# Three inner Strassen products per pair instead of two, in the four FFNs of a fused two-block kernel

## The chip, the cores and the metric

One core of one Trainium2 chip runs the whole kernel: an execution is one launch of one program. The metric is device time in microseconds. TensorE multiplies, VectorE, ScalarE and GpSimd work on tiles in SBUF (VectorE and ScalarE also in PSUM, where TensorE writes), and SyncE's and ScalarE's queues issue the transfers from HBM. All data are float32. The profile records each matmul as two instructions: four matmuls of 128x256, one product of the text, show as "x8".

## The reference, cut to what matters

Two blocks act on `x` of 512 tokens by 1024 features. The first is FFN, a mixer of attention and pooling, FFN; the second has two layers, each a mixer (attention with selected keys, then a state space model) and a convolved FFN. The change touches the four FFNs, here FFN0 to FFN3:

```
def swiglu(x, w1, w3, w2):
    return (jax.nn.silu(x @ w1) * (x @ w3)) @ w2
...
    h = h + 0.5 * swiglu(rms_norm(h, ffn1_norm[l]), ffn1_w1[l], ffn1_w3[l], ffn1_w2[l])
...
def conv_ffn(h, w_up, conv_w, conv_b, w_down):
    up = h @ w_up
    up = lax.conv_general_dilated(
        up, conv_w[:, None, :], window_strides=(1,), padding=[(CONV_W - 1, 0)],
        dimension_numbers=('NWC', 'WIO', 'NWC'), feature_group_count=2 * D_FF) + conv_b
    val, gate = jnp.split(up, 2, axis=-1)
    return (jax.nn.silu(gate) * val) @ w_down
```

FFN0 and FFN1 are `swiglu`, FFN2 and FFN3 `conv_ffn` with `CONV_W = 3`. The inner width `D_FF` is 2816. The second block also needs `silu(c) @ ada_w + ada_b` for its scales; that work lies in FFN0 and FFN1.

## The kernel before, in words

**The up projection by Strassen.** Everything is stored with features on the partitions. An FFN's 2816 columns (22 tiles of 128, `FC`) are taken in `NP = 11` pairs `p`. A pair has two weight slots `w`: `w = 0` and `w = 1` hold 256 columns of each of the two up matrices (or halves of `w_up`). Each slot's product with the tokens is a 2 by 2 block product in Strassen's form (Winograd's variant), so seven products `"P1"` to `"P7"` in place of eight; an outer product is `KC // 2 = 4` matmuls of a 128x128 weight block with 256 tokens. The sums of weight blocks that it needs (`combine`, four of 128x512 a slot, L624 to L629) are GpSimd's. The sums of token blocks (`h_mix_dve`) are made once for an FFN.

**The second level.** From the second pair on, two outer products of both slots share their tokens, so P6 (called `w = 2`) and P7 (`w = 3`), each for both slots at once, are again 2 by 2 products and again done by seven: an inner product is two matmuls with 128 tokens (`inner`, L746). Their weight sums are four of 128x256 each for GpSimd (`combine` with `inner_left`), their token sums `t1` to `t4` are VectorE's, once an FFN (`h_inner_mix`). P4 of both slots stays outer: two products of four matmuls.

**VectorE puts the results together.** In the first pair by `first_step` 1 to 5 for each slot, after that by `pair_step` 1 to 20, which read PSUM and add into the tiles `u` (P1 of both slots, copied by ScalarE as `first(p, w)`) and `act_t` (`quadrants`). Steps 1 to 8 need the first four inner products of each kind, and ScalarE's copies of the first inner products (`inner_copy_act`). TensorE's `(2, "P2")` waits for step 4, `(3, "P2")` for step 8. Each step adds one to the semaphore `quad`.

**Behind the steps** come, in FFN0 and FFN1, ScalarE's silu and two `product`s into `gT` (L1013, L1016) and four `ada_slab_dve` a pair, each a 128x1024 multiply and sum for the second block's scales (L1348). In FFN2 and FFN3 a pair has four tiles; each gets a `base` tap on ScalarE (L2599) and two more taps on VectorE (`earlier`, L2637 and L2640), then a silu and `product` (L2646). The taps of slot 0 are held in PSUM in pairs 1 to 9, those of slot 1 in SBUF (`rs`, `acc`).

**The down projection** (`strassen_down_pe`, L836) is Strassen's too in FFN0, FFN1 and FFN3. It needs four sums of the gated tiles of each pair `r` (`g_mix_dve`, L940 to L945): for pairs 0 to 7 they are made within the up projection, after the pair's last product; for pairs 8 to 10 behind it (`g_mix_last_dve`). FFN2 has a plain down projection (`down_pe`). The down weights of one quarter come in three slots (`GROUPS`: four, four and three pairs). For each slot TensorE does P1, P6, P7 and P5, then the next slot's.

**The weights** stream through a ring of four slots of 1 MB. A pair uses two; a slot is loaded anew when TensorE has passed the event in `FREES`, here `(w, "P3")` of its pair. Then GpSimd waits for the load and combines. The order of TensorE's products within a pair is written out by hand in `pair_steps`, that of the other engines in the functions named above; all meet through counting semaphores.

## Time and profile before

| what | value |
|---|---|
| median of 3 runs | 2671.56 us (2663.66 to 2671.83) |
| profiled execution, its own time | 2669.95 us |
| its span, first to last instruction | 2668.2 us |
| mean granted TensorE clock | 0.983 |
| busy TensorE | 2578.8 us, 97% |
| busy VectorE | 1681.1 us, 63% |
| busy GpSimd | 1232.2 us, 46% |
| busy ScalarE | 595.9 us, 22% |
| read from HBM | 255.14 MB |

The times are those of whole executions; the profile is of one of them, and the span leaves out what lies around the first and the last instruction. Busy shares are averages over stages, so a share says how full an engine is, not who waits for whom; the timeline and the waits say that.

### The profile page before, as it was taken

Reading aid. Unit: us, or ns where it says so; the run is one execution under the profiler, and the core shown is the slowest. Engines: PE = TensorE matmul, PEld = TensorE weight load, DVE = VectorE, ACT = ScalarE, POOL = GpSimd, SP = SyncE. Lnnn points to the kernel's source line nnn. Section 1 sums busy time; section 2 is a strip of 40 time slices with the busy share of each in tenths; the row PEclk is TensorE's granted clock in tenths of the full one; section 3 lists DMA queues with packets and bytes.
Section 4 is the critical chain, followed back from the end, with each engine's and each line's share of the span. In section 5 each row is a group of like instructions: output and inputs, shape, how many; then the busy total and the mean of one; then the engine's idle time right before and its main releaser. Section 6 shows DMA issues by size and latency. Waiting matters only on the chain.

```text
span 2668.2 us, 33470 instructions
## 1 busy us (share of the span) xinstructions
PE 2578.8 (97%) x12942; PEld 2056.1 (77%) x12942; DVE 1681.1 (63%) x2859; ACT 595.9 (22%) x1172; POOL 1232.2 (46%) x1128
## 2 busy tenths in 40 slices
PE   7999999999999999999999989999999699999999
PEld 6999889888467889886654567999644567899888
DVE  6776512588656887523498765677652875788721
ACT  2111001432201111002235642222202621222200
POOL 6666532440435677440000254677031884677642
PEclk9999999999999999999999999999999799999999
DMA  6555422221124555421122012223330422122222
GB/s 205 182 189 170 158 87 79 95 64 64 48 71 139 175 166 181 156 89 53 48 63 79 17 32 72 75 91 104 105 86 11 148 91 79 64 95 95 91 78 68
DMA packets 244062, 264.26 MB, mean 99 GB/s; under 512 B 31744, under 2 KB 226112, under 8 KB 243776
## 3 DMA queue, kind: packets, MB, share of 16 engines
q1 hardware_dynamic: 227968, 206.89, 24.5%
q10 hardware_dynamic: 15936, 55.22, 5.9%
q8 instruction: 104, 1.70, 0.3%
q14 instruction: 54, 0.44, 0.1%
HBM read 255.14 MB, written 6.29 MB: 98 GB/s over the span
## 4 chain that ended last, share of the span: by engine, by line
PE 88%; DVE 6%; POOL 2%; issue 2%; ACT 1%; DMA 0%; SPq 0%; DVEq 0%; ACTq 0%
PE ps L791 27%; PE ps L836 14%; PE ps L746 9%; PE ps L1615 6%; PE ps L589 6%; PE ps L2203 5%; PE ps L1434 3%; PE ps L3213 3%; PE ps L2238 2%; PE ps L1588 1%; PE ps L1744 1%; PE ps L1575 1%; POOL phase L3469 1%; PE ps L1158 1%; PE ps L2251 1%
## 5 line engine op out<-in xcount | busy, mean ns | idle before, releaser
L791 PE MATMUL ps<-hT,ring 128*128 128x256 f32 x2176 | 505.0, 381 | 7.9 <-DVE phase L1013 4.7
L791 PEld LDWEIGHTS ps<-hT,ring 128*128 128x128 f32 x2176 | 411.2, 191 | 67.5 <-issue 9.1
L624 POOL TENSOR_TENSOR ring<-ring 128x512 f32<-128x512 f32 (+1 forms) x124 | 168.7, 1360 | 552.5 <-DMA ring<-in_ffn_w 301.1
L836 PE MATMUL ps<-phase,ring 128*128 128x256 f32 x1848 | 400.1, 379 | 1.6 <-DVE phase L945 1.5
L836 PEld LDWEIGHTS ps<-phase,ring 128*128 128x128 f32 x1848 | 351.2, 190 | 50.0 <-DVE phase L945 2.3
L791 PE MATMUL ps<-phase,ring 128*128 128x256 f32 x1472 | 349.2, 381 | 6.2 <-DVE act_t L856 5.5
L791 PEld LDWEIGHTS ps<-phase,ring 128*128 128x128 f32 x1472 | 274.5, 191 | 41.6 <-DVE act_t L856 6.7
L627 POOL TENSOR_TENSOR ring<-ring 128x512 f32<-128x512 f32 (+2 forms) x204 | 237.6, 1165 | 0.0
L2561 POOL TENSOR_SCALAR phase<-phase 128x128 f32<-128x128 f32 (+3 forms) x64 | 33.4, 535 | 334.9 <-DVE phase L2530 334.9
L626 POOL TENSOR_TENSOR ring<-ring 128x512 f32<-128x512 f32 (+1 forms) x124 | 167.7, 1353 | 9.7
L629 POOL TENSOR_TENSOR ring<-ring 128x512 f32<-128x512 f32 (+1 forms) x124 | 171.1, 1380 | 0.0
L589 PE MATMUL ps<-phase,ring 128*128 128x512 f32 x352 | 152.3, 593 | 0.0
L882 DVE TENSOR_TENSOR act_t<-act_t,ps 128x128 f32<-128x128 f32 (+1 forms) x320 | 102.1, 349 | 69.1 <-PE ps L791 66.2
L2203 PE MATMUL ps<-hT,ring 128*128 128x512 f32 x320 | 140.1, 593 | 1.0 <-ACT hT L1310 0.5
L589 PEld LDWEIGHTS ps<-phase,ring 128*128 128x128 f32 x352 | 66.5, 190 | 81.5 <-issue 81.3
L2203 PEld LDWEIGHTS ps<-hT,ring 128*128 128x128 f32 x320 | 60.7, 190 | 78.0 <-issue 76.4
L1434 PE MATMUL ps<-phase,ring 128*128 128x256 f32 x448 | 99.4, 384 | 3.7 <-DVE phase L1404 3.6
L1348 DVE CUSTOM_DVE_ANT_0 phase<-phase,ps,vcol 128x1024 f32<-128x1024 f32 x80 | 101.9, 1273 | 0.0
L1615 PE MATMUL ps<-phase,ring 128*128 128x256 f32 x448 | 101.3, 379 | 0.0
L1434 PEld LDWEIGHTS ps<-phase,ring 128*128 128x128 f32 x448 | 86.0, 192 | 17.2 <-DVE phase L1404 4.5
L746 PE MATMUL ps<-phase,ring 128*128 128x128 f32 x640 | 96.1, 278 | 2.0 <-DVE u L882 2.0
L882 DVE TENSOR_TENSOR act_t<-u,ps 128x256 f32<-128x256 f32 (+1 forms) x120 | 44.9, 374 | 83.2 <-PE ps L791 52.2
(451 smaller groups left out, 4403.5 us busy)
## 6 DMA issues: line engine op xcount, KB each, us to landing
ring<-in_ffn_w SPq DMA_DIRECT2D x60, 1024.0 KB, 5.4
phase<-in_ada_w ACTq DMA_DIRECT2D x96, 512.0 KB, 3.5
ring<-in_ffn_w_up SPq DMA_DIRECT2D x44, 1024.0 KB, 5.0
ring<-in_w_in SPq DMA_DIRECT2D x19, 1024.0 KB, 5.2
ring<-in_attn_w_in SPq DMA_DIRECT2D x14, 1024.0 KB, 5.2
ring<-in_ffn_w_down SPq DMA_DIRECT2D x8, 1408.0 KB, 6.3
ring<-in_ssm_w_glu SPq DMA_DIRECT2D x8, 1024.0 KB, 5.7
ring<-in_ffn_w_down SPq DMA_DIRECT2D x8, 1024.0 KB, 5.1
```

The lines of the kernel that those rows point to most:

```text
L589: mm = pe.matmul(ps[:, (q % 2) * 2 + t, :], wtile(nd + 2 * q + s, c, FC // 2, t * P, (t + 1) * P), gT[:, f * T:(f + 1) * T], start=(f == 0 ...
L624: pool.tensor_tensor(s1, a21, a22, ALU.add).then_inc(combined, 1)
L626: pool.tensor_tensor(s2, s1, a11, ALU.subtract).then_inc(combined, 1)
L627: pool.tensor_tensor(a21, a11, a21, ALU.subtract).then_inc(combined, 1)
L629: pool.tensor_tensor(s4, a12, s2, ALU.subtract).then_inc(combined, 1)
L746: mm = pe.matmul(ps[:, inner_bank(w), at:at + P], left[:, c], tokens[:, c], start=(name == "P1" and c == 0), stop=(c == 1), skip_group_che ...
L791: mm = pe.matmul(ps[:, 4 * w + bank_of[name], 0:HALF], left[:, c], right[name](c), start=(opens and c == 0), stop=(c == KC // 2 - 1), skip ...
L836: mm = pe.matmul(ps[:, bank_of[name], 0:HALF], left[:, r - lo], right(name, r), start=(half == 0 and r == 0), stop=(r == NP - 1), skip_gro ...
L882: dve.tensor_tensor(dst, x, y, ALU.add).then_inc(quad, 1)
L1434: mm = pe.matmul(ps[:, out_bases(q) + banks[name], 0:HALF], left[:, c], right(name, c), start=(name in ("P1", "P6", "P7", "P5") and c == 0 ...
L1615: mm = pe.matmul(ps[:, bank, 0:HALF], left[:, c], right[name](c), start=(name in ("P1", "P6", "P7", "P5") and c == 0), stop=(c == KC // 2 ...
L2203: mm = pe.matmul(out, wtile(n, c, KC, t * P, (t + 1) * P), src(c), start=(c == 0), stop=(c == KC - 1))
```

## The change

The other products with shared tokens, P4 of both slots, become a third inner product (`w = 4`) from the second pair on. It takes PSUM bank 1, which the first inner product (`w = 2`) also uses, so each waits for VectorE's reads of the other. Its tokens are the outer token sum `t4` in `hx[:, 2]`; its own token sums are GpSimd's, once an FFN (`h_inner_last_pool`), its weight sums four more of 128x256 a pair. A pair has 25 steps: 17 to 21 and 24, 25 place the third product, two of the old steps go. Both slots of a pair are now freed by its very last product, `(4, "P3")`.

The other engines' orders change with it. In the first pair the token sums of the inner products are spread between the steps. The sums of gated tiles are made in pairs 3, 5, 7 and 9 for pairs 0 to 3, and for pairs 4 to 10 behind the up projection; TensorE waits for them at P6 instead of P1. Two of the four slabs of the first pair move to the down projection's second quarter. In FFN2 and FFN3 the taps are done tile by tile, that of `(w, i) = (0, 0)` before step 23 and the other three behind step 25. The rotation table's operations in FFN1 are spread one to a pair.

```diff
-INNER = (2, 3)
+INNER = (2, 3, 4)
...
-    order = [(0, "P1"), (1, "P1")] + [(w, name) for w in INNER for name in ("P1", "P6", "P7", "P5")]
-    order += [(0, "P5"), (0, "P2")] + [(2, name) for name in ("P2", "P4", "P3")] + [(1, "P5")]
-    order += [(3, name) for name in ("P2", "P4", "P3")]
-    return order + [(1, "P2"), (0, "P4"), (0, "P3"), (1, "P4"), (1, "P3")]
+    opening, closing = ("P1", "P6", "P7", "P5"), ("P2", "P4", "P3")
+    order = [(0, "P1"), (1, "P1")] + [(w, name) for w in (2, 3) for name in opening]
+    order += [(0, "P5"), (0, "P2")] + [(2, name) for name in closing] + [(1, "P5"), (1, "P2")]
+    order += [(3, name) for name in closing] + [(4, name) for name in opening]
+    return order + [(0, "P3"), (1, "P3")] + [(4, name) for name in closing]
...
-                put(n + 2 * b + w, e + EVENTS[k]["up", b, w, "P3"])
+                put(n + 2 * b + w, e + EVENTS[k]["up", b, 4 if b else w, "P3"])
...
+        def h_inner_last_pool(pool, k):
+
+            b11, b12, b21, b22 = inner_right(4)
+            t1, t2, t4 = inner_sums(k, 4)[0]
+            pool.wait_ge(h_mixed, 4 * k + 4)
+            pool.tensor_tensor(t1, b12, b11, ALU.subtract).then_inc(last_mixed, 1)
+            pool.wait_ge(last_mixed, 4 * k + 1)
+            pool.tensor_tensor(t2, b22, t1, ALU.subtract).then_inc(last_mixed, 1)
+            pool.wait_ge(last_mixed, 4 * k + 2)
+            pool.tensor_tensor(t4, b21, t2, ALU.subtract).then_inc(last_mixed, 1)
+            pool.wait_ge(tile_done, TILE0[f"ffn{k}"] + EVENTS[k]["up", 0, 1, "P4"])
+            pool.tensor_tensor(b12, b22, b12, ALU.subtract).then_inc(last_mixed, 1)
...
                             for r in range(lo, hi):
                                 if q == 0 and name == "P1":
+                                    pe.wait_ge(gated, FC * k + 2 * r + 2)
+                                if q == 0 and name == "P6":
                                     pe.wait_ge(g_mixed, G_MIXED0[k] + 4 * (r + 1))
...
-            if step in (17, 19):
-                w = (step - 17) // 2
-                done(w, "P4")
-                add(g[w], g[w], ps[:, 4 * w, 0:HALF])
-            if step in (18, 20):
-                w = (step - 18) // 2
+            if step == 17:
+                dve.wait_ge(in_copied, copies + 3)
+                add(v4, v4, inner(4, 3, 4))
+            if step == 18:
+                after(17)
+                add(g[0][:, P:], g[0][:, P:], v4)
+            if step == 19:
+                x = g[1].rearrange("p (s t) -> p s t", s=2)
+                add(x, x, v4.unsqueeze(1).to_broadcast([P, 2, P]))
+            if step in (20, 21):
+                after(step - 1)
+                add(g[1][:, P:], g[1][:, P:], inner(4, 2, 3) if step == 20 else inner(4, 1, 2))
+            if step in (22, 23):
+                w = step - 22
                 done(w, "P3")
                 add(quadrants[w][:, HALF:2 * HALF], halves[:, w, :], ps[:, 4 * w + 3, 0:HALF])
+            if step == 24:
+                done(4, "P3")
+                add(g[0], g[0], inner(4, 0, 2))
+            if step == 25:
+                add(g[1][:, 0:P], g[1][:, 0:P], inner(4, 2, 3))
...
+        G_MIX_AT = (3, 5, 7, 9)
+
         def g_mix_last_dve(dve, k):
 
-            dve.wait_ge(tile_done, TILE0[f"ffn{k}"] + EVENTS[k]["up", NP - 1, 1, "P4"])
-            for r in range(8, NP):
+            dve.wait_ge(tile_done, TILE0[f"ffn{k}"] + EVENTS[k]["up", NP - 1, 4, "P3"])
+            for r in range(len(G_MIX_AT), NP):
                 g_mix_dve(dve, k, r)
...
-        SLAB_BEHIND = (8, 9, 16)
+        SLAB_BEHIND = (8, 9, 21, 25)
...
-                for step in range(9, 19):
+                for step in range(12, 23):
                     pair_step(dve, k, p, step)
-                earlier(p, 0)
-                pair_step(dve, k, p, 19)
-                pair_step(dve, k, p, 20)
-            earlier(NP - 1, 1)
+                tile_taps(p, 0, 0)
+                for step in range(23, 26):
+                    pair_step(dve, k, p, step)
+                tile_taps(p, 1, 0)
+            for w in range(2):
+                tile_taps(NP - 1, w, 1)
+            product(NP - 1, 0)
             product(NP - 1, 1)
-            product(NP - 1, 0)
```

Three places show how the instructions now stand. The first is TensorE's queue at the end of a pair of FFN0, before: behind P2 of slot 1 come P4 and P3 of slot 0, P4 and P3 of slot 1, each four matmuls.

```order
L791 MATMUL ps<-hT,ring 128x256 [waits first_products_copied]
L791 MATMUL ps<-hT,ring 128x256 x3
L791 MATMUL ps<-phase,ring 128x256 [waits silu_done]
L791 MATMUL ps<-phase,ring 128x256 x3
L791 MATMUL ps<-hT,ring 128x256 [waits weights_combined,quadrant_steps]
L791 MATMUL ps<-hT,ring 128x256 x3
L791 MATMUL ps<-phase,ring 128x256 [waits gated]
L791 MATMUL ps<-phase,ring 128x256 x3
L791 MATMUL ps<-hT,ring 128x256 [waits weights_combined,quadrant_steps]
L791 MATMUL ps<-hT,ring 128x256 x3
```

And now: the end of the third inner product's opening (its P7 and P5), P3 of both slots, and its closing P2, P4 and P3 (two matmuls each).

```order
L774 MATMUL ps<-phase,ring 128x128 [waits weights_combined]
L774 MATMUL ps<-phase,ring 128x128
L774 MATMUL ps<-sq,acc 128x128 [waits weights_combined]
L774 MATMUL ps<-sq,acc 128x128
L814 MATMUL ps<-hT,ring 128x256 [waits weights_combined,quadrant_steps]
L814 MATMUL ps<-hT,ring 128x256 x3
L814 MATMUL ps<-hT,ring 128x256 [waits weights_combined,quadrant_steps]
L814 MATMUL ps<-hT,ring 128x256 x3
L774 MATMUL ps<-phase,ring 128x128 [waits quadrant_steps]
L774 MATMUL ps<-phase,ring 128x128
L774 MATMUL ps<-acc,ring 128x128 x2
```

What moved: both outer P4 left, and an inner P2 that waits for step 21 stands between the last outer product and the pair's end.

The second place is VectorE's queue at the end of a pair of FFN2, before: steps 17 and 18, the four taps of slot 0 (in PSUM), steps 19 and 20, the four taps of slot 1.

```order
L882 TENSOR_TENSOR act_t<-act_t,ps 128x256 [waits tile_done]
L882 TENSOR_TENSOR act_t<-u,ps 128x256 [waits tile_done]
L2637 SCALAR_TENSOR_TENSOR ps<-act_t,vcol,ps 128x511 [waits conv_base]
L2640 SCALAR_TENSOR_TENSOR ps<-act_t,vcol,ps 128x510 [waits conv_taps]
L2637 SCALAR_TENSOR_TENSOR ps<-act_t,vcol,ps 128x511 [waits conv_base]
L2640 SCALAR_TENSOR_TENSOR ps<-act_t,vcol,ps 128x510 [waits conv_taps]
L882 TENSOR_TENSOR act_t<-act_t,ps 128x256 [waits tile_done]
L882 TENSOR_TENSOR act_t<-u,ps 128x256 [waits tile_done]
L2637 SCALAR_TENSOR_TENSOR rs<-act_t,vcol,rs 128x511 [waits conv_base]
L2640 SCALAR_TENSOR_TENSOR rs<-act_t,vcol,rs 128x510 [waits conv_taps]
L2637 SCALAR_TENSOR_TENSOR acc<-act_t,vcol,acc 128x511 [waits conv_base]
L2640 SCALAR_TENSOR_TENSOR acc<-act_t,vcol,acc 128x510 [waits conv_taps]
```

And now: step 22, one tile's taps, steps 23 to 25, and then three tiles' taps; two rows of products follow in both orders.

```order
L914 TENSOR_TENSOR act_t<-u,ps 128x256 [waits tile_done]
L2703 SCALAR_TENSOR_TENSOR ps<-act_t,vcol,ps 128x511 [waits conv_base]
L2706 SCALAR_TENSOR_TENSOR ps<-act_t,vcol,ps 128x510 [waits conv_taps]
L914 TENSOR_TENSOR act_t<-u,ps 128x256 [waits tile_done]
L914 TENSOR_TENSOR act_t<-act_t,ps 128x256 [waits tile_done]
L914 TENSOR_TENSOR act_t<-act_t,ps 128x128
L2703 SCALAR_TENSOR_TENSOR acc<-act_t,vcol,acc 128x511 [waits conv_base]
L2706 SCALAR_TENSOR_TENSOR acc<-act_t,vcol,acc 128x510 [waits conv_taps]
L2703 SCALAR_TENSOR_TENSOR ps<-act_t,vcol,ps 128x511 [waits conv_base]
L2706 SCALAR_TENSOR_TENSOR ps<-act_t,vcol,ps 128x510 [waits conv_taps]
L2703 SCALAR_TENSOR_TENSOR rs<-act_t,vcol,rs 128x511 [waits conv_base]
L2706 SCALAR_TENSOR_TENSOR rs<-act_t,vcol,rs 128x510 [waits conv_taps]
```

What moved: behind the last step that reads the pair's last product there stood four taps, now six.

The third place is VectorE's queue where FFN0's up projection ends, before: the last step, the last product, the four sums of pair 8; those of pairs 9 and 10 follow in the same pattern.

```order
L882 TENSOR_TENSOR act_t<-u,ps 128x256 [waits tile_done]
L1016 TENSOR_TENSOR phase<-act_t 128x768 [waits quadrant_steps,silu_done]
L940 TENSOR_TENSOR phase<-phase 128x256 [waits gated,tile_done]
L942 TENSOR_TENSOR phase<-phase 128x256 [waits gated_combined]
L943 TENSOR_TENSOR phase<-phase 128x256
L945 TENSOR_TENSOR phase<-phase 128x256 [waits gated_combined]
```

And now: steps 24 and 25, a slab, the last product, the sums of pair 4; those of pairs 5 to 10 follow.

```order
L914 TENSOR_TENSOR act_t<-act_t,ps 128x256 [waits tile_done]
L914 TENSOR_TENSOR act_t<-act_t,ps 128x128
L1404 ISA phase,mod<-phase,ps,vcol 128x1024 [waits slab_loaded2]
L1404 ISA mod 128x1
L1068 TENSOR_TENSOR phase<-act_t 128x768 [waits quadrant_steps,silu_done]
L985 TENSOR_TENSOR phase<-phase 128x256 [waits gated,tile_done]
L987 TENSOR_TENSOR phase<-phase 128x256 [waits gated_combined]
L988 TENSOR_TENSOR phase<-phase 128x256
L990 TENSOR_TENSOR phase<-phase 128x256 [waits gated_combined]
```

What moved: the sums behind the up projection are 28 operations instead of 12, and a slab stands ahead of them.

## Rows read from the trace of the kernel before

**Rows 1.** The page, part 1: busy time, share of the span, instructions of each engine.

```profile
PE 2578.8 (97%) x12942; PEld 2056.1 (77%) x12942; DVE 1681.1 (63%) x2859; ACT 595.9 (22%) x1172; POOL 1232.2 (46%) x1128
```

**Rows 2.** Timeline of TensorE, two pairs of FFN0: start us, us, engine, line.

```profile
56.46 0.61 PE L746 MATMUL ps<-phase,ring 128*128 128x128 f32 x4
...
60.03 1.89 PE L791 MATMUL ps<-phase,ring 128*128 128x256 f32 x8
61.76 1.89 PE L791 MATMUL ps<-hT,ring 128*128 128x256 f32 x8
...
79.98 0.61 PE L746 MATMUL ps<-phase,ring 128*128 128x128 f32 x4
```

**Rows 3.** The same view, first pairs of FFN0, FFN1 (two), FFN3.

```profile
46.18 3.61 PE L791 MATMUL ps<-phase,ring 128*128 128x256 f32 x8 [2.84 <-DVE act_t L856]
...
859.03 3.36 PE L791 MATMUL ps<-hT,ring 128*128 128x256 f32 x8 [3.31 <-DVE phase L1013]
...
893.82 0.71 PE L746 MATMUL ps<-phase,ring 128*128 128x128 f32 x4 [0.89 <-DVE u L882]
...
2288.93 1.99 PE L791 MATMUL ps<-phase,ring 128*128 128x256 f32 x8 [1.34 <-DVE act_t L856]
```

**Rows 4.** Busy time by window: from:to, us, engines, clock, DMA share, GB/s.

```profile
46.20:49.60 3.40, 3.40 (x8) 2.77 (x9) 2.62 (x3) 0.00 (x0) 3.32 (x3) 0.52 0.01 2
```

**Rows 5.** Timeline of TensorE, one pair of FFN2.

```profile
1691.33 0.61 PE L746 MATMUL ps<-phase,ring 128*128 128x128 f32 x4
...
1715.07 0.61 PE L746 MATMUL ps<-phase,ring 128*128 128x128 f32 x4
...
1722.20 1.16 PE L746 MATMUL ps<-phase,ring 128*128 128x128 f32 x8
```

**Rows 6.** Timeline of VectorE, FFN0 (first two) and FFN2.

```profile
66.70 1.48 DVE L882 TENSOR_TENSOR act_t<-u,rs 128x128 f32<-128x128 f32 x2
...
278.38 0.48 DVE L882 TENSOR_TENSOR act_t<-u,rs 128x128 f32<-128x128 f32 x2
...
1712.95 0.75 DVE L2637 SCALAR_TENSOR_TENSOR rs<-act_t,vcol,rs 128x511 f32<-128x511 f32 x1 [0.61 <-ACT rs L2599]
1713.74 1.64 DVE L2640 SCALAR_TENSOR_TENSOR rs<-act_t,vcol,rs 128x510 f32<-128x510 f32 x1
...
1718.65 0.68 DVE L2646 TENSOR_TENSOR phase<-ps,rs 128x512 f32<-128x512 f32 x1
```

**Rows 7.** Timeline of GpSimd, FFN0 (first two) and FFN2.

```profile
267.93 1.26 POOL L626 TENSOR_TENSOR ring<-ring 128x512 f32<-128x512 f32 x1
269.15 1.26 POOL L627 TENSOR_TENSOR ring<-ring 128x512 f32<-128x512 f32 x1
...
1728.21 0.73 POOL L624 TENSOR_TENSOR const<-ring 128x256 f32<-128x256 f32 x1
```

**Rows 8.** The page, part 6: DMA issues, count, KB each, us to landing.

```profile
ring<-in_ffn_w_up SPq DMA_DIRECT2D x44, 1024.0 KB, 5.0
```

**Rows 9.** Timeline, TensorE, GpSimd, VectorE: FFN0 passes to its down projection.

```profile
288.21 57.14 PE L836 MATMUL ps<-phase,ring 128*128 128x256 f32 x264
...
289.60 1.15 POOL L624 TENSOR_TENSOR ring<-ring 128x384 f32<-128x384 f32 x1 [12.61 <-DMA ring<-in_ffn_w]
...
289.81 1.22 DVE L940 TENSOR_TENSOR phase<-phase 128x256 f32<-128x256 f32 x1
...
294.37 1.49 DVE L940 TENSOR_TENSOR phase<-phase 128x256 f32<-128x256 f32 x1
...
300.00 0.41 DVE L940 TENSOR_TENSOR phase<-phase 128x256 f32<-128x256 f32 x1
...
301.46 1.28 DVE L1348 CUSTOM_DVE_ANT_0 phase<-phase,vcol 128x1024 f32<-128x1024 f32 x1
```

**Rows 10.** The same of TensorE and VectorE at the end of FFN3.

```profile
2545.18 0.70 PE L836 MATMUL ps<-phase,ring 128*128 128x256 f32 x2 [0.70 <-DVE phase L945]
...
2536.73 1.76 DVE L2646 TENSOR_TENSOR phase<-sq,rs 128x512 f32<-128x512 f32 x1
```

More of the change, by code:

```diff
@@ L631, in combined_up @@
         def combined_up(k, p, w, step):
-            return COMBINED0[k] + (8 + 16 * (p - 1) if p else 0) + 4 * w + step
+            return COMBINED0[k] + (8 + 20 * (p - 1) if p else 0) + 4 * w + step
         def inner_left(k, p, w):
             pair = [SLOT0[f"ffn{k}"] + 2 * p + j for j in range(2)]
-            x, y = (mixes(n, KC // 2)[1] if w == 2 else up_blocks(n)[2] for n in pair)
+            x, y = (mixes(n, KC // 2)[1] if w == 2 else up_blocks(n)[w - 1] for n in pair)
             return x[:, 0:2], x[:, 2:4], y[:, 0:2], y[:, 2:4]
@@ L2617, in strassen_conv_act @@
                 if p == 0:
-                    base(p, 0)
+                    base(p, 0, 1)
+                    base(p, 0, 0)
                 last(p, 1)
-                if p >= 1:
-                    base(p, 0)
-                base(p, 1)
+                if p == 0:
+                    base(p, 1, 1)
+                    base(p, 1, 0)
+                else:
+                    inner_copy_act(act, k, p, 4)
+                    for i in range(2):
+                        for w in range(2):
+                            base(p, w, i)
@@ L2643, in product @@
             def product(p, i):
[L2644 to L2645 removed]
+                dve.wait_ge(taps, TAPS * l + 8 * p + 2 * tap_place(p, 0, i) + 2)
+                dve.wait_ge(silu_done, p0 + 2 * p + (1 if (i == 1) == (p == 0) else 2))
                 dve.tensor_tensor(gT[:, (2 * p + i) * T:(2 * p + i + 1) * T], conv_tile(p, 0, i), convolved[1][i],
@@ L2650, in strassen_conv_dve @@
                 first_step(dve, k, 0, step)
-            h_inner_dve(dve, k, ("t1", "t2", "t4"))
-            earlier(0, 0)
-            for step in range(1, 6):
-                first_step(dve, k, 1, step)
-            h_inner_dve(dve, k, ("t3",))
-            for p in range(1, NP):
-                earlier(p - 1, 1)
-                product(p - 1, 1)
-                product(p - 1, 0)
-                for step in range(1, 9):
+            first_step(dve, k, 1, 1)
+            h_inner_dve(dve, k, ("t1",))
@@ new lines, in strassen_conv_dve @@
+            first_step(dve, k, 1, 2)
+            tile_taps(0, 0, 1)
+            first_step(dve, k, 1, 3)
+            tile_taps(0, 0, 0)
+            first_step(dve, k, 1, 4)
+            h_inner_dve(dve, k, ("t2",))
+            first_step(dve, k, 1, 5)
+            h_inner_dve(dve, k, ("t3", "t4"))
+            for p in range(1, NP):
+                if p == 1:
+                    tile_taps(0, 1, 1)
+                    for step in range(1, 5):
+                        pair_step(dve, k, p, step)
+                    tile_taps(0, 1, 0)
+                    for step in range(5, 9):
+                        pair_step(dve, k, p, step)
+                    product(0, 1)
+                    product(0, 0)
+                else:
+                    for w in range(2):
+                        tile_taps(p - 1, w, 1)
+                    product(p - 1, 0)
+                    product(p - 1, 1)
+                    for step in range(1, 9):
+                        pair_step(dve, k, p, step)
+                for step in range(9, 12):
@@ L2669, in strassen_conv_dve @@
-            earlier(NP - 1, 1)
+                tile_taps(p, 0, 0)
+                for step in range(23, 26):
+                    pair_step(dve, k, p, step)
+                tile_taps(p, 1, 0)
+            for w in range(2):
+                tile_taps(NP - 1, w, 1)
+            product(NP - 1, 0)
             product(NP - 1, 1)
-            product(NP - 1, 0)
             if k in STRASSEN_DOWN:
```

234 lines of the change are left out of this document (130 added, 104 removed).

## The prediction

> **What bounds the kernel now.** I read first the busy times on the page: TensorE is busy in 97% of the span [rows 1]. So the kernel is a row of products, and a change counts by what it takes out of TensorE's own time and by the waits that it makes or removes there. Next the timeline of TensorE over two pairs of the first FFN: an outer product (eight instructions of 128x256) takes 61.76 - 60.03 = 1.73 us, eight inner products take 60.03 - 56.46 = 3.57 us, 0.446 each, and a pair repeats after 79.98 - 56.46 = 23.52 us [rows 2]. That is 10 outer and 14 inner products and nothing else: in a middle pair of this FFN TensorE waits for nobody. Then I looked for its waits (the idle times in brackets on the timeline). They lie in the first two pairs of each FFN [rows 3], as a small step before `(2, "P2")` in each pair of the two FFNs with the convolution [rows 5], and where the last of these FFNs passes to its down projection [rows 10].
>
> **The change, part by part. The products.** Two outer P4, 3.46 us, become seven inner products, 3.12 us: 0.34 us less in each of 40 pairs, **-13.6 us**.
>
> **Waits that go.** Before, VectorE did the eight inner token sums ahead of, or between, the steps for which `(1, "P4")` and the next `(1, "P1")` wait. Now steps come first, and two of a pair's four slabs move away. In FFN0 that ends waits of 2.84 (shown) and 1.42 us [rows 3]; after the longer one the granted clock was 0.52 [rows 4], the lower level of 1.2 GHz, so that eight matmuls took 3.61 instead of 1.89 us. Together 6.0 us. In FFN1 the wait of 3.31 us and its slow product (3.36 for 1.89) are 4.8 us; the product of gates there still stands behind two sums that GpSimd slows, so I take 4.1. FFN1's second and fourth pair lose waits of 0.89 (shown) and 1.06 us, with their starts 2.2, since sums of gated tiles and the steps of the rotation table no longer meet there. FFN2 and FFN3 lose 1.34 us each (one is shown), 2.9 with the starts. The conv pairs take 1715.07 - 1691.33 = 23.74 us, 0.22 above the bare products, 3.5 us in 16 pairs [rows 5]. Sum **-18.7 us**.
>
> **The third inner product's own work.** GpSimd gets four sums of 128x256 more per pair, at 0.73 us each 2.9 us [rows 7]. It may start them only when the pair before is over, when it would idle until new weights land (5.0 us after their issue [rows 8]): hidden, as is its later start now that both slots are freed at the pair's end. VectorE's steps 17 to 21 must lie between the inner P5 (18.4 us after a pair's start) and the inner P2 (21.8). Copy and handover take about 0.5, three adds from PSUM about 0.8; the two adds with both operands in SBUF take 0.48 together when GpSimd rests and 1.48 when it works [rows 6]. That ends at 21.2: no wait, with 0.6 to spare, in all FFNs. If GpSimd were then in its long sums, it would be late by about 0.8.
>
> **The conv pairs.** Here the chain is long. Before, the taps after a pair's end are four operations of 128x511, one free at 0.75, three beside GpSimd at (1718.65 - 1713.74)/3 = 1.64 [rows 6], and end at 1718.65; `(2, "P2")` starts at 1722.20 [rows 5], 3.55 later (products, step 1 to 4). Pair start is 1715.07 - 3.45 = 1711.62, so taps end 7.0 after it and P2 could have gone at 10.5. Now six operations stand behind the end. Steps 17 to 21 delay step 22, its base tap on ScalarE and the first tile's taps (1.5), so step 25 ends 1.6 after the pair's end, the next base tap at 1.9. Then two taps beside GpSimd's third inner sums (between 0.75 and 1.4 each), two into PSUM at 0.75, two beside the outer sums, of which the first may still slip in free. That ends between 7.0 and 8.9; plus 3.55 it is 10.5 to 12.5, for a product due at 10.47. I take 11.7: a wait of 1.2 us in 17 pairs (not in the first conv pairs, and not in FFN2's last, where GpSimd has no outer sums), **+20.4 us**; ends 0 and 2.0, so 0 to +34.
>
> **The sums behind the up projection.** This is what speaks most against the change. A pair's four sums take 301.46 - 300.00 = 1.46 us alone, but 294.37 - 289.81 = 4.56 beside the combinations of 128x384 and 300.00 - 294.37 = 5.63 beside those of 128x512 [rows 9]. By the Trainium skill, page "SBUF — State Buffer", section "Who interferes with whom", the second to start blocks fully until the first finishes; the trace agrees that they hinder each other. By the rule an operation of 0.36 alone and a combination of 1.22 alone [rows 7, 9] would take 1.58 together, against 5.63/4 = 1.41 in the rows; eight of them would cost 1.4 us more at each end. The sum goes by the rows. Before, 12 such operations stood there, needed 13.8 us after the end, and were done at 301.46 - 288.21 = 13.2. Now 28 do, and P6 of the second slot needs the sums of pairs 4 to 7: P1, P6, P7, P5 of the first group and P1 of the second are five times four matmuls of 1.73/4 = 0.43, so pair 4 is due at 8.6 and pair 7 at 9.9. VectorE is free at 1.60 + 1.28 (a slab now stands ahead) + 0.2 = 3.1. Pair 4's end at 4.5. GpSimd's combinations start from 4.8: before, 1.39 after the end for a slot freed 3.46 ahead of it; the next slot's, issued right behind, follow without a gap. Eight of the twelve other operations are slowed: pair 6 is done at 13.5, pair 7 at 16.0. TensorE is through P6 at 16.5 instead of 10.4: 6.1 us, and about 1 more for the lower clock, which the wait of 4 us should bring as in [rows 4]. Twice (FFN0, FFN1) 14.2. In FFN3 taps and products come first (beside GpSimd a product takes up to 1.76 [rows 10], and its combinations stretch to some 1.4 and 1.7 as well); six taps and two products end at 10.7, pair 4's sums at 16.3, pair 7's at 20.7: 10.7, less the 0.70 (shown) and 0.76 of before [rows 10], plus 1: 10.2. Sum **+24.4 us**; if GpSimd rested, pair 7 would be done at 8.9 and only FFN3 would wait, about 3.5, so +2 is the low end; +32 the high one.
>
> **The sum.** -13.6 - 18.7 + 20.4 + 24.4 = +12.5 us. The profiled execution took 2669.95 us (span 2668.2), 1.6 below the median of 2671.56. I forecast 2671.56 + 12.5 = **2684 us**. 0.3%, 8 us, is about what a measurement of this kernel can tell from no change.
>
> **The rivals.** (a) *The conv chain fits.* A longer pause of GpSimd, or taps that start first, let steps 1 to 4 end in time; for it, the tap that starts ahead of GpSimd is free in [rows 6]; against it, two more taps stand after the end. Without that term: -7.9 us, **2664**. Under 0.7 us per pair it decides. 18%. (b) *The sums behind the projection are in time*, because the second load lands late and leaves VectorE alone; against it, the combinations follow without a gap in [rows 9]. The end term falls to about 5: -7 us, **2665**; 10%. (c) Both: -13.6 - 18.7 + 5 = -27, **2644**, 12%. The other side of zero needs one of these. (d) *Third inner product late in every pair*: long sums of GpSimd lie beside steps 18 and 19; 0.8 us in 20 pairs of FFN0 and FFN1, **2700**; for it, contention at these adds [rows 6]; against it, GpSimd should be in the short sums by then. 8%. (e) The forecast, 2674 to 2694 as its own range: 52%.
>
> **How the numbers follow.** From (a), (b) and (c) 8, 6 and 12% lie below -8 us: faster 0.26. Within 8 us are the rest of (a) and (b), 14%, and the low edge of (e), 9%: same 0.23. Slower 0.51. The range, leaving out (c)'s low half and (d)'s upper: 2652 to 2702.
>
> **What would show it.** TensorE's rows: inner pattern of 12 after the last P3, pair of 23.2 us in FFN0; there no idle of 2.84 or 3.31 in the first pairs. In the conv FFNs an idle before `(2, "P2")` of about 1.2 released by a VectorE add into u; if it is below 0.3, (a). In the first 17 us of the down projections waits on the sums, 6 us in two FFNs and over 10 in the last; if they are missing, (b). I am wrong if GpSimd's combinations there start much later than 4.8 us after the end, or if VectorE's steps 17 to 21 start late.

## The result and the profile after

The changed kernel takes 2688.07 us (median of 5 runs, 2682.77 to 2693.51), the kernel before 2671.56 in the same comparison (2663.66 to 2672.67). The ratio is 1.0065, with a 95% interval of 1.0042 to 1.0088: slower by 0.65%. The forecast was 2684.

The profiled execution of the changed kernel is the slowest of its five, 2693.51 us with a span of 2691.6, so it stands 23.4 us above the span of before where the medians stand 16.5 apart. Part 1 of its page, against [rows 1]:

```profile
PE 2577.1 (96%) x13422; PEld 2066.5 (77%) x13422; DVE 1734.1 (64%) x3059; ACT 604.3 (22%) x1212; POOL 1365.7 (51%) x1304
```

TensorE is busy for 1.7 us less than before, in a span that is 23.4 us longer: the change brought waits, and slower products behind them. To place them I cut both traces at TensorE's rows. "Up" is the time from an FFN's first outer product to the first product of its down projection; "end" is the time from there to VectorE's first update of `xT`, for which the down projection's first P1 and P6 must be complete.

| us | FFN0 up | end | FFN1 up | end | FFN2 up | FFN3 up | end |
|---|---|---|---|---|---|---|---|
| before | 268.40 | 17.13 | 267.49 | 17.12 | 263.90 | 264.44 | 19.50 |
| after | 258.75 | 24.06 | 257.72 | 23.01 | 266.27 | 277.93 | 29.80 |
| difference | -9.65 | +6.93 | -9.77 | +5.89 | +2.37 | +13.49 | +10.30 |

The seven differences add up to +19.6 of the 23.4. The rest lies outside these stretches and cannot be told from what moves from run to run: the stretch from FFN1's first update to FFN2's first product takes 527.5 us here and 523.6 before, and lies between 520.2 and 527.5 in the ten other kernels below.

**FFN0 and FFN1.** TensorE's timeline shows no idle time in any pair, and a pair repeats after 23.19 us in place of 23.52 [rows 2]; the waits of [rows 3] are gone. What follows the up projection of FFN0, on TensorE, then the busy times and the granted clock over the 24.06 us, and over the products behind the wait:

```profile
278.40 10.09 PE L867 MATMUL ps<-phase,ring 128*128 128x256 f32 x46
292.43 7.74 PE L867 MATMUL ps<-phase,ring 128*128 128x256 f32 x22 [3.93 <-DVE phase L990]
...
278.40:302.46 24.06, 20.13 (x82) 16.97 (x81) 21.57 (x37) 1.23 (x2) 10.04 (x8) 0.86 0.41 137
...
292.43:300.20 7.77, 7.77 (x23) 6.43 (x24) 7.46 (x14) 0.00 (x0) 2.48 (x2) 0.64 0.00 0
```

L990 is the fourth sum of `g_mix_dve`. TensorE gets through 23 matmuls (46 records) and then stands for 3.93 us. The kernel before did the same work (81 records, here 82) busy and at clock 1.00:

```profile
288.21:305.34 17.13, 17.13 (x81) 15.10 (x80) 14.55 (x18) 0.38 (x1) 10.04 (x8) 1.00 0.38 130
```

So the end costs 3.93 us of waiting and 20.13 - 17.13 = 3.0 us of slow products: behind the wait the granted clock is 0.64 on average, between the two levels of 1.2 and 2.4 GHz.

**The conv pairs.** One pair of FFN3: TensorE with the wait for an add into `u` (steps 2 to 4), VectorE with the taps behind the pair's end, and GpSimd's first outer sums.

```profile
2417.61 3.62 PE L814 MATMUL ps<-hT,ring 128*128 128x256 f32 x16
...
2430.03 0.71 PE L774 MATMUL ps<-phase,ring 128*128 128x128 f32 x4 [1.78 <-DVE u L914]
...
2419.40 1.22 DVE L2703 SCALAR_TENSOR_TENSOR acc<-act_t,vcol,acc 128x511 f32<-128x511 f32 x1 [0.40 <-ACT acc L2650]
2420.66 1.10 DVE L2706 SCALAR_TENSOR_TENSOR acc<-act_t,vcol,acc 128x510 f32<-128x510 f32 x1
2421.68 0.74 DVE L2703 SCALAR_TENSOR_TENSOR ps<-act_t,vcol,ps 128x511 f32<-128x511 f32 x1
...
2423.12 1.77 DVE L2703 SCALAR_TENSOR_TENSOR rs<-act_t,vcol,rs 128x511 f32<-128x511 f32 x1
2424.93 1.64 DVE L2706 SCALAR_TENSOR_TENSOR rs<-act_t,vcol,rs 128x510 f32<-128x510 f32 x1
2426.49 0.68 DVE L2712 TENSOR_TENSOR phase<-ps,acc 128x512 f32<-128x512 f32 x1
...
2423.07 1.27 POOL L630 TENSOR_TENSOR ring<-ring 128x512 f32<-128x512 f32 x1 [1.86 <-DMA ring<-in_ffn_w_up]
```

GpSimd starts 0.05 us ahead of the first tap into `rs`, and both taps take more than twice the 0.75 of a free one. In FFN2 the first of the two often slips in free:

```profile
1787.65 0.74 DVE L2703 SCALAR_TENSOR_TENSOR rs<-act_t,vcol,rs 128x511 f32<-128x511 f32 x1
1788.43 1.64 DVE L2706 SCALAR_TENSOR_TENSOR rs<-act_t,vcol,rs 128x510 f32<-128x510 f32 x1
...
1788.21 1.31 POOL L630 TENSOR_TENSOR ring<-ring 128x512 f32<-128x512 f32 x1 [1.34 <-DMA ring<-in_ffn_w_up]
```

Of the nine distances between pair starts in FFN2, four are 23.55 to 23.76 us, one is 24.25 and one 23.19 (the first two and the last 25.06 to 25.33); in FFN3 eight are 25.06 to 25.80 and one is 23.44. In FFN3 sums of gated tiles stand in every second pair as well. In the first such pair the tap into `rs` was free and the wait at P2 short, but an add behind the sums was late:

```profile
2352.26 0.71 PE L774 MATMUL ps<-phase,ring 128*128 128x128 f32 x4 [0.79 <-DVE u L914]
...
2361.73 3.72 PE L814 MATMUL ps<-hT,ring 128*128 128x256 f32 x16 [1.29 <-DVE act_t L914]
```

The waits behind the sums are 1.29, 1.28, 0.15 and 0.16 us in the four pairs. And both conv FFNs have two waits in the first conv pair that I had not seen coming, here FFN2's:

```profile
1672.42 0.71 PE L774 MATMUL ps<-phase,ring 128*128 128x128 f32 x4 [0.60 <-DVE u L914]
1679.44 0.71 PE L774 MATMUL ps<-phase,ring 128*128 128x128 f32 x4 [0.60 <-DVE u L914]
```

**The end of FFN3** has four waits for the same sums, the first two long; before it were 0.70 and 0.76 [rows 10].

```profile
2557.55 1.19 PE L867 MATMUL ps<-phase,ring 128*128 128x256 f32 x2 [5.91 <-DVE phase L990]
2559.99 1.22 PE L867 MATMUL ps<-phase,ring 128*128 128x256 f32 x2 [1.25 <-DVE phase L990]
```

### The profile page after: what moved, and what is told of

Its sections match the earlier page's. It is cut to its first block, busy times and chain, and to the rows that moved or that the text cites. A ratio compares the mean times of both kernels' runs of the same rounds, so it can differ in the third digit from the quotient of the medians.

```text
span 2691.6 us, 34964 instructions
## 1 busy us (share of the span) xinstructions
PE 2577.1 (96%) x13422; PEld 2066.5 (77%) x13422; DVE 1734.1 (64%) x3059; ACT 604.3 (22%) x1212; POOL 1365.7 (51%) x1304
## 3 DMA queue, kind: packets, MB, share of 16 engines
q8 instruction: 108, 1.77, 0.3%
## 4 chain that ended last, share of the span: by engine, by line
PE 77%; DVE 15%; ACT 3%; POOL 2%; issue 2%; DMA 0%; DVEq 0%; ACTq 0%; SPq 0%
PE ps L814 16%; PE ps L867 14%; PE ps L774 11%; PE ps L1671 6%; PE ps L595 6%; PE ps L2255 5%; PE ps L1490 3%; PE ps L3299 3%; DVE act_t L914 2%; PE ps L2290 2%; DVE u L914 1%; PE ps L1644 1%; DVE rs L2706 1%; PE ps L1800 1%; PE ps L1631 1%
## 5 line engine op out<-in xcount | busy, mean ns | idle before, releaser
L867 PE MATMUL ps<-phase,ring 128*128 128x256 f32 x1848 | 409.3, 385 | 15.5 <-DVE phase L990 15.5
L867 PEld LDWEIGHTS ps<-phase,ring 128*128 128x128 f32 x1848 | 355.8, 193 | 68.1 <-DVE phase L990 12.6
L630 POOL TENSOR_TENSOR ring<-ring 128x512 f32<-128x512 f32 (+1 forms) x124 | 163.6, 1319 | 383.6 <-DMA ring<-in_ffn_w 219.4
L633 POOL TENSOR_TENSOR ring<-ring 128x512 f32<-128x512 f32 (+2 forms) x244 | 267.8, 1098 | 0.0
L814 PE MATMUL ps<-phase,ring 128*128 128x256 f32 x832 | 195.5, 379 | 0.9 <-DVE phase L682 0.9
L774 PE MATMUL ps<-phase,ring 128*128 128x128 f32 x1040 | 157.1, 277 | 19.6 <-DVE u L914 19.3
L632 POOL TENSOR_TENSOR ring<-ring 128x512 f32<-128x512 f32 (+1 forms) x124 | 163.7, 1321 | 9.7
L774 PEld LDWEIGHTS ps<-phase,ring 128*128 128x128 f32 x1040 | 143.1, 191 | 32.5 <-DVE u L914 27.2
L814 PEld LDWEIGHTS ps<-phase,ring 128*128 128x128 f32 x832 | 151.8, 190 | 18.6 <-issue 1.3
L635 POOL TENSOR_TENSOR ring<-ring 128x512 f32<-128x512 f32 (+1 forms) x124 | 164.1, 1324 | 0.0
L595 PEld LDWEIGHTS ps<-phase,ring 128*128 128x128 f32 x352 | 66.4, 190 | 81.5 <-issue 80.8
L914 DVE TENSOR_TENSOR act_t<-act_t,ps 128x128 f32<-128x128 f32 (+1 forms) x400 | 116.0, 322 | 14.8 <-PE ps L774 9.1
L1490 PE MATMUL ps<-phase,ring 128*128 128x256 f32 x448 | 100.6, 387 | 3.7 <-DVE phase L1460 3.7
L1671 PE MATMUL ps<-phase,ring 128*128 128x256 f32 x448 | 101.3, 379 | 0.0
L1490 PEld LDWEIGHTS ps<-phase,ring 128*128 128x128 f32 x448 | 86.8, 194 | 17.6 <-DVE phase L1460 4.5
```

The lines of the kernel that those rows point to most:

```text
L595: mm = pe.matmul(ps[:, (q % 2) * 2 + t, :], wtile(nd + 2 * q + s, c, FC // 2, t * P, (t + 1) * P), gT[:, f * T:(f + 1) * T], start=(f == 0 ...
L630: pool.tensor_tensor(s1, a21, a22, ALU.add).then_inc(combined, 1)
L632: pool.tensor_tensor(s2, s1, a11, ALU.subtract).then_inc(combined, 1)
L633: pool.tensor_tensor(a21, a11, a21, ALU.subtract).then_inc(combined, 1)
L635: pool.tensor_tensor(s4, a12, s2, ALU.subtract).then_inc(combined, 1)
L774: mm = pe.matmul(ps[:, inner_bank(w), column:column + P], left[:, c], tokens[:, c], start=(name == "P1" and c == 0), stop=(c == 1), skip_g ...
```

## The experiments

Ten kernels ran, in three groups; each group has its own runs of the kernel before, and ratios are to those. The stages of each:

| us | FFN0 up | end | FFN1 up | end | FFN2 up | FFN3 up | end | median | ratio to before (95%) |
|---|---|---|---|---|---|---|---|---|---|
| e1 sums in the up projection | 258.74 | 17.14 | 262.98 | 17.13 | 267.85 | 276.17 | 28.99 | 2679.45 | 1.004 (1.0027 to 1.0053) |
| e2 products behind step 8 | 258.75 | 22.95 | 256.79 | 23.02 | 261.05 | 267.48 | 29.87 | 2673.68 | 1.0013 (1.0002 to 1.0024) |
| e3 narrow GpSimd sums | 258.73 | 22.93 | 257.57 | 22.93 | 257.54 | 257.55 | 29.19 | 2657.25 | 0.996 (0.9945 to 0.9975) |
| e4 GpSimd waits for taps | 258.74 | 24.54 | 256.80 | 23.95 | 262.58 | 266.77 | 30.15 | 2673.41 | 1.0022 (1.0012 to 1.0032) |
| f1 all mended | 258.74 | 17.13 | 256.79 | 17.13 | 257.54 | 257.86 | 24.35 | 2639.70 | 0.9892 (0.9877 to 0.9907) |
| f2 before, GpSimd waits | 269.90 | 17.13 | 268.40 | 17.13 | 262.41 | 263.00 | 19.41 | 2666.30 | 0.999 (0.9978 to 1.0001) |
| f3 e2 and e4 | 258.75 | 24.10 | 256.80 | 22.92 | 257.54 | 264.62 | 29.76 | 2665.99 | 0.9988 (0.9977 to 0.9999) |
| f4 before, sums late | 268.38 | 23.93 | 265.79 | 23.82 | 264.16 | 264.32 | 27.88 | 2688.49 | 1.0074 (1.0061 to 1.0088) |
| g1 f1 without the hold | 258.75 | 17.13 | 257.76 | 17.13 | 257.54 | 257.89 | 28.21 | 2643.12 | 0.9902 (0.9883 to 0.9921) |
| g3 token sums on VectorE | 260.29 | 17.13 | 256.88 | 17.13 | 257.68 | 258.06 | 24.15 | 2644.49 | 0.9913 (0.9895 to 0.993) |

### e1: sums back in the up projections of FFN0 and FFN1

```diff
 def strassen_silu_dve ...
-                if p in G_MIX_AT:
-                    g_mix_dve(dve, k, G_MIX_AT.index(p))
+                if p < 8:
+                    g_mix_dve(dve, k, p)
 def g_mix_last_dve ...
-            for r in range(len(G_MIX_AT), NP):
+            for r in range(8 if k < 2 else len(G_MIX_AT), NP):
```

> The changed kernel, but in FFN0 and FFN1 the gated tiles of pairs 0 to 7 are summed at the end of their own pairs again (three pairs stay behind the up projection); FFN3 is left as changed. Theory A, the sums behind the up projection cost a wait of TensorE and the low clock behind it, and VectorE has room for them in the pairs: the 3.93 us wait in each of FFN0 and FFN1 goes and the 22 products behind it take 4.75 us again instead of 7.74; the stretches from the end of the up projection to the next FFN fall back by 8.2 and 9.8 us, the pairs stay at 23.19 us; total -14 to -18, near 2672. Rival B, the pairs are full with three products: each of the eight pairs with sums gets 0.5 to 1.5 us longer and eats the gain; total within 5 us of 2688. Rival C, the wait was not from the sums but from the late last steps of the pair (step 25, product): the wait of 3.93 us stays.

Both ends went back to 17.14 and 17.13, to a hundredth what they are in the kernel before, and in FFN0 the up projection lost nothing. TensorE behind the up projection of FFN0, and its window:

```profile
278.70 21.53 PE L867 MATMUL ps<-phase,ring 128*128 128x256 f32 x99
...
278.70:296.00 17.30, 17.30 (x83) 15.23 (x82) 11.85 (x21) 1.23 (x2) 10.25 (x8) 1.00 0.58 195
```

Theory A holds for the ends and for FFN0, with one exception that has a row. In FFN1 the first pair's sums stand ahead of steps 1 to 4 of the second pair, the first with inner products, all four beside GpSimd, together with an operation of the rotation table (L2143):

```profile
859.12 0.71 PE L774 MATMUL ps<-phase,ring 128*128 128x128 f32 x4 [3.40 <-DVE u L914]
...
849.88 1.38 DVE L985 TENSOR_TENSOR phase<-phase 128x256 f32<-128x256 f32 x1
851.29 1.38 DVE L987 TENSOR_TENSOR phase<-phase 128x256 f32<-128x256 f32 x1
852.59 1.49 DVE L988 TENSOR_TENSOR phase<-phase 128x256 f32<-128x256 f32 x1
854.00 1.49 DVE L990 TENSOR_TENSOR phase<-phase 128x256 f32<-128x256 f32 x1
855.41 1.48 DVE L2143 CAST const<-const 128x512 f32<-128x512 int32 x1
```

That wait and the slow products behind it made one pair 28.5 us long and gave 5.3 us back. So the total came to 2679.45 us, 1.004 of before where the change has 1.0065, and not to the 2672 that I expected. Part of what FFN1 gained in the change came from taking the first pair's sums out of this place, and not from the new order of steps; f4, which moves the sums in the kernel before, shortens FFN1's up projection by 1.7 us. The sums need not leave the up projection, only this place: in f1 they stand at the ends of pairs 2 to 9 and cost nothing there.

### e2, e4 and f3: the chain in the conv pairs

e2 takes VectorE's products out of the chain. ScalarE's copies move ahead of the second SiLU (not shown here).

```diff
 def strassen_conv_dve ...
                     for w in range(2):
                         tile_taps(p - 1, w, 1)
-                    product(p - 1, 0)
-                    product(p - 1, 1)
                     for step in range(1, 9):
                         pair_step(dve, k, p, step)
+                    product(p - 1, 0)
+                    product(p - 1, 1)
```

> The changed kernel, but in pairs 2 to 10 of FFN2 and FFN3 VectorE does steps 1 to 8 of a pair ahead of the two gate products of the pair before, and ScalarE copies the first inner products ahead of the second SiLU. Theory A, the wait of TensorE at each pair's first P2 is the length of VectorE's chain (four late taps, two products, steps 1 to 4): 1.5 us of products and the 0.17 for the SiLU leave the chain, the waits of 1.75 to 1.87 us fall under 0.4, pairs go from 25.2 to about 23.6; FFN2's up projection 266.3 to about 263, FFN3's 277.9 to about 266, total about -15, near 2673. Rival B, VectorE is full in these pairs: the same work done in another order moves the wait to a later product of the pair (the second or third inner group) and the pairs stay near 25.2; total within 4 us of 2688.

e4 leaves the order and delays GpSimd.

```diff
 def combine_pool ...
                     pool.wait_ge(w_loaded[n % RING], 16 * (n // RING + 1))
+                    if k >= 2 and p >= 2 and w == 0:
+                        pool.wait_ge(taps, TAPS * (k - 2) + 8 * (p - 1))
```

> The changed kernel, but in FFN2 and FFN3 (from pair 2 on) GpSimd starts a pair's outer sums only when VectorE's last taps of the tiles of two pairs before are done, some 3.4 us later than now in FFN3. Theory A, two rhythms (with the sums' start just ahead of or behind the first rs tap): taps at 0.75 us, the wait at P2 from 1.8 to 0.4 us or less, pairs of 23.2 to 23.6 us; FFN3's up projection 277.9 to 266 to 268, FFN2's 266.3 to 264, total -10 to -14. Rival B, the collision only moves: VectorE's steps 1 to 8 and GpSimd's first sums now slow each other, the wait stays over 1 us, total within 3 us of 2688. Rival C, GpSimd's sums come too late for the first inner products: TensorE waits on GpSimd, total over 2690.

f3 has both edits.

> The changed kernel with both conv edits together (products behind step 8, GpSimd's outer sums behind the late taps), its sums of gated tiles untouched. Theory A, the two causes add: FFN2's up projection falls to 257.5 to 259 (every pair 23.19), FFN3's to 264 to 267 (23.19 without sums, 25.2 in the four pairs with sums), total about 2670. Rival B, they are one and the same saving: FFN2 stays at 261 to 262.6 and the total at 2673.

Each edit alone takes much of the wait away (FFN3's up projection 277.9 to 267.5 and 266.8, FFN2's 266.3 to 261.1 and 262.6; f3 has 264.6 and 257.5), and rival B of e2 and e4 falls. In e2 the taps are as slow as in the change and only the chain is shorter, in e4 they are fast. First e2, then e4 (taps into `rs`, the next slow add, GpSimd):

```profile
2409.18 1.69 DVE L2703 SCALAR_TENSOR_TENSOR rs<-act_t,vcol,rs 128x511 f32<-128x511 f32 x1
...
2414.79 0.71 PE L774 MATMUL ps<-phase,ring 128*128 128x128 f32 x4 [0.47 <-DVE u L914]
```

```profile
2407.12 0.74 DVE L2705 SCALAR_TENSOR_TENSOR rs<-act_t,vcol,rs 128x511 f32<-128x511 f32 x1
2407.90 0.75 DVE L2708 SCALAR_TENSOR_TENSOR rs<-act_t,vcol,rs 128x510 f32<-128x510 f32 x1
...
2410.41 1.43 DVE L916 TENSOR_TENSOR u<-u,extra 128x384 f32<-128x384 f32 x1
...
2419.01 0.29 DVE L916 TENSOR_TENSOR act_t<-u,ps 128x128 f32<-128x128 f32 x1 [3.18 <-PE ps L776]
...
2439.53 1.48 DVE L987 TENSOR_TENSOR phase<-phase 128x256 f32<-128x256 f32 x1
...
2443.76 0.94 DVE L992 TENSOR_TENSOR phase<-phase 128x256 f32<-128x256 f32 x1
...
2408.80 1.28 POOL L630 TENSOR_TENSOR ring<-ring 128x512 f32<-128x512 f32 x1 [2.44 <-DVE rs L2708]
```

In e4 part of the collision does move, to step 2 (1.43 us, against 1.02 in the change and 0.56 in e3), but that is one operation made slower for two made fast. With both edits every pair of FFN2 takes 23.19 us and its up projection 257.54: theory A of f3. The remainder in FFN3, 264.62 - 257.54 = 7.1 us, lies in the pairs that hold sums of gated tiles (24.66 to 25.06 us, the others 23.19). The rows of e4 show why: the four sums run from 2439.53 to 2444.7, 5.2 us, where VectorE has a gap of 3.18 in a pair without them.

### e3: GpSimd's share

```diff
 def combine ...
+            narrow = any(COMBINED0[k] + 8 <= i < COMBINED0[k] + COMBINED_UP for k in (2, 3))
+            if narrow:
+                blocks, sums = ([x[:, :, 0:8] for x in b] for b in (blocks, sums))
```

> The changed kernel, but in pairs 1 to 10 of FFN2 and FFN3 GpSimd's sums of the weight blocks cover 8 of the 128 columns (the rest of each sum is left out). Theory A, the late taps are slow because GpSimd works in SBUF beside them: the rs taps fall from 1.77 and 1.64 us to about 0.75, the acc taps from 1.22 and 1.10 to about 0.75, the chain gets 2.7 us shorter and the wait at P2 goes: FFN3's up projection 277.9 to 264 to 266, FFN2's 266.3 to about 261 to 263, total -15 to -20. Rival B, the order alone makes the wait: taps keep their times, total within 3 us of 2688.

All pairs of both conv FFNs fall to 23.19 us with the order of the change untouched, the sums of gated tiles in FFN3 included. A tap of VectorE's chain:

```profile
2393.28 0.74 DVE L2706 SCALAR_TENSOR_TENSOR rs<-act_t,vcol,rs 128x511 f32<-128x511 f32 x1
```

This kernel leaves out 120 of the 128 columns of each sum, so its time is a bound and not a gain to be had. VectorE's work in its new order would fit; what makes it late is GpSimd's work beside it. The 257.5 is also the floor for the other runs, 6.4 and 6.9 us under the kernel before: that is what the change could gain there.

### f4: the late sums alone, in the kernel before

Two inner products as before, but `G_MIX_AT = (3, 5, 7, 9)`, seven pairs' sums behind the up projection, and `(q 0, "P1")` waiting for `gated` alone.

> The kernel before, with the sums of gated tiles placed as the change places them (four pairs' sums inside, seven behind the up projection; TensorE's first products wait only for the gated tile), and two inner products as before. Theory A, the end costs the same without the third inner product: first residual update 6 to 8 us later in FFN0 and FFN1 and 10 later in FFN3, FFN3's up projection shorter by at most 1 us; total +20 to +24, near 2691. Rival B, most of the cost at the end comes from the third inner product's late last steps: +3 us or less at each end, total within 10 us of before.

The ends come 6.8, 6.7 and 8.4 us later, and the total rises by 18 us, a little under what theory A gave. This one part, without the third inner product, costs as much as the whole change (0.74% against 0.65%); all else in the change about cancels.

The price is much the same as in the change, but not the rows. Here GpSimd starts 1.5 us after FFN0's up projection has ended (6.3 in the change, where both slots are freed at the pair's very end), so that pair 4's sums are slow as well and the wait stands earlier, at 299.81 - 287.89 = 11.9 us against 14.0:

```profile
289.41 1.02 POOL L624 TENSOR_TENSOR ring<-ring 128x384 f32<-128x384 f32 x1 [12.24 <-DMA ring<-in_ffn_w]
...
299.81 1.22 PE L838 MATMUL ps<-phase,ring 128*128 128x256 f32 x2 [2.69 <-DVE phase L947]
```

### f2: the kernel before, with GpSimd waiting

The edit of e4 in the kernel before.

> The kernel before, with one edit: in FFN2 and FFN3 (from pair 2 on) GpSimd's outer sums wait for VectorE's late taps. Theory A, before had the same collision but TensorE's 0.2 us a pair is all it cost there: up projections of FFN2 and FFN3 263.9 and 264.4 to 261.5 to 262.5 (23.52 a pair), total -3 to -4. Rival B, no change (the 0.2 us has another cause): within 1 us. Rival C, GpSimd is late for before's order: slower by over 3 us.

From the second conv pair on they all take 23.52 us in place of 23.73 (one 24.10); FFN2 gains 1.5 and FFN3 1.4 us in these stages, as theory A has it. FFN0 and FFN1, which the edit does not touch, took 1.5 and 0.9 us more in this profile, so the total, 0.1% down with an interval that reaches 1.0001, cannot be told from no change.

### f1 and g1: everything mended

f1 has e2 and e4, the sums of pairs 0 to 7 in FFN0 and FFN1 at the ends of pairs 2 to 9, and in FFN3 halves of sums in pairs 2 to 10. At FFN3's end GpSimd is held.

```diff
 def strassen_silu_dve ...
+                if 2 <= p < 10:
+                    g_mix_dve(dve, k, p - 2)
 def strassen_conv_dve ...
+                if k in STRASSEN_DOWN and p >= 2:
+                    g_mix_dve(dve, k, (p - 2) // 2, p % 2)
 def combine_pool ... (down slots)
+                        if k == 3 and (q, g) in ((0, 2), (1, 0)):
+                            pool.wait_ge(g_mixed, G_MIXED0[k] + (24 if q == 0 else 4 * NP))
```

> The changed kernel with every cost found so far mended: FFN0 and FFN1 make the sums of pairs 0 to 7 again inside the up projection (at the ends of pairs 2 to 9); in FFN2 and FFN3 VectorE's products stand behind step 8 and GpSimd's outer sums wait for the late taps; FFN3's sums come in halves of two instructions in pairs 2 to 10; and at the end of FFN3's up projection GpSimd holds its sums of the down slots back behind VectorE's sums of pairs 4 and 5, and 4 to 10. Theory A (each cost has its own place and they add): first residual update 17.1 us behind the up projection in FFN0 and FFN1 (23 to 24 in the changed kernel), FFN2's up projection 258 to 260 and FFN3's 258 to 261 (266.3 and 277.9), first residual update of FFN3 24 to 27 us behind the up projection (29.8); total 2645 to 2655, faster than before by about 0.7%. Rival B, the halves still cost 1 us a pair beside GpSimd's sums and the held sums come late for TensorE: FFN3's up projection 265 or more, its end not shorter; total 2658 or more.

2639.70 us, 1.1% faster than before and 5 us better than the low edge I gave. FFN3's pairs with halves take 23.19 us (one 23.52). Its end is 4.9 us above before, since six and a half pairs' sums are still there. VectorE in f1 at that end, its product and one sum with GpSimd held and one beside it:

```profile
2499.83 0.69 DVE L2718 TENSOR_TENSOR phase<-sq,acc 128x512 f32<-128x512 f32 x1
...
2502.76 0.42 DVE L994 TENSOR_TENSOR phase<-phase 128x256 f32<-128x256 f32 x1
...
2504.90 1.21 DVE L994 TENSOR_TENSOR phase<-phase 128x256 f32<-128x256 f32 x1
```

g1 is f1 without the hold.

> The mended kernel of the run f1_all_mended without one of its edits: GpSimd's sums of the down slots at the end of FFN3's up projection start as soon as the slots have landed. Theory A, VectorE's closing sums are slow beside them: VectorE's two products take 1.4 to 1.5 us again instead of 0.69 and its first sums 1.2 to 1.5 instead of 0.42, the first residual update of FFN3 comes 28 to 30 us behind the up projection instead of 24.35, total +4 to +5, near 2644. Rival B, the halves of the sums (half of pair 4's made inside) gained it: the update stays within 1 us of 24.35.

The end is 28.21 us again and VectorE's product 1.48:

```profile
2502.21 1.48 DVE L2716 TENSOR_TENSOR phase<-sq,rs 128x512 f32<-128x512 f32 x1
```

So the hold is worth 3.9 us in the trace, and rival B falls. The medians of f1 and g1 differ by 3.4, across two groups of runs.

### g3: the token sums on VectorE

> The mended kernel of the run f1_all_mended with the third inner product's four token sums in each FFN on VectorE, behind its own token sums of the first pair, instead of on GpSimd. Theory A, VectorE is the late engine in the openings and the sums cost there what they take, 4 times 0.5 to 1.5 us: TensorE waits 2 to 5 us in the first or second pair of each FFN, up projections of FFN0 258.7 to 261 or more and of FFN2 257.5 to 260 or more, total +6 to +16. Rival B, VectorE's room in the first pair (it waits for TensorE's products there) holds them: total within 2 us of 2640.

FFN0's up projection takes 1.55 us more (one wait of 1.27), FFN1 to FFN3 0.1 to 0.2. That is between the two theories and nearer to B: GpSimd is the better place in FFN0 alone. The median is 4.8 us above that of f1, from another group; the stages account for only some 2 of them, and the two intervals overlap.

## Why the prediction was right

The direction, slower, to which I had given 51%, and the time (2684 against 2688.07) came out. By its own terms, measured in the profiled execution:

- **The products**: -0.34 forecast, -0.33 measured per pair (23.52 to 23.19), -13.3 us. Right.
- **Waits that go**: -18.7 forecast. FFN0 6.3 and FFN1 6.4 beyond the products (6.0 and 6.3 forecast); FFN2 and FFN3 together 6.6, from the floor of e3 (6.4 forecast). Right in size. For FFN1's wait of 3.31 us the step named the token sums alone; e1 shows that with the new order a wait of 3.40 is there again if the first pair's sums stay where they were.
- **Steps 17 to 21**: no wait, as forecast; rival (d) is out, since the pairs of FFN0 and FFN1 take 23.19 us.
- **The conv chain**: +20.4 forecast. Measured against the floor, FFN2 +8.7, FFN3 +20.4, together 29.1. If the sums are put at 7.1, as f3 has them, 22.0 are left. The mechanism was the right one, and e3 and e4 show it. The even 1.2 us per pair was not: FFN2 lost 0.4 to 0.6 in four of nine pairs and about 2 in three, FFN3 1.9 to 2.6 in eight (its sums included), as GpSimd starts just behind or just ahead of the tap into `rs`. In the 22.0 stand also the two waits of the first conv pair, a pair that I had left out: 25.06 - 23.19 = 1.9 us in each FFN, so that the 17 pairs of the forecast are left with some 18.3.
- **A term that was missing**: the sums of gated tiles inside FFN3's pairs. I moved them from eight pairs to four and costed those at nothing. In e4 they take 5.2 us in a gap of about 3.2, and in f3 they cost 7.1 us. That is their price when the chain's own wait is gone. In the changed kernel TensorE's waits right behind them are 2.9 us in all, so how the 29.1 divide between chain and sums there is not shown.
- **The sums behind the up projection**: +24.4 forecast, 6.9 + 5.9 + 10.3 = 23.1 measured. The sum is right, its parts are not, and that they made up for each other is luck. In FFN0 I had 6.1 us of wait and 1 of clock, and the rows have 3.93 and 3.0; in FFN1 they have 3.93 and 2.0; in FFN3 I had 9.2 of wait beyond before's and 1 of clock, and the rows have 6.2 and 4.1. In FFN0 and FFN1 GpSimd's combinations started 6.3 us after the end (284.71 - 278.40, the row below), and not 4.8, which I had named as a sign of being wrong; so only pair 7 was late. The clock cost two to four times what I took from the short stretch of [rows 4]. The price of a sum held: beside the 128x512 combinations they again start 1.4 us apart.

```profile
284.71 1.17 POOL L630 TENSOR_TENSOR ring<-ring 128x384 f32<-128x384 f32 x1 [11.53 <-DMA ring<-in_ffn_w]
```

Together -13.3 - 19.3 + 22.0 + 7.1 + 23.1 = +19.6 against +12.5; the medians stand 16.5 apart. The prediction was right by its mechanisms, and the conv pairs, chain and missing term together, are what it had too low: 29.1 against 20.4.

## What to carry to other kernels

Moving work behind a stage so that the stage fits is paid for at once where the next stage needs it: here the late sums alone cost 18 us (f4), more than half of the 33 that the products and the waits gave, although in FFN0 and FFN1 VectorE had room for them in the pairs from the third on (f1). Look for the gap that a block of work must fit in, with the other engine's slowing counted, and cut the block to the gap before moving it away (f1 does it in FFN3). And where two engines slow each other, ask which of the two has slack: one wait on GpSimd, which had time, was worth as much as a reordering of VectorE (2673.41 and 2673.68 us).
